# The distance bias made at the start of the program and read back one stage earlier, with the pooling sums placed inside the attention stage

## The chip, the cores and the metric

The kernel runs on one core of a Trainium2 chip. All numbers are fp32. The metric is the device time of one execution in microseconds (us). TensorE does the matrix products (PE in the profile, PEld its weight loads), VectorE (DVE) the elementwise work and the selection, ScalarE (ACT) the activations and the copies out of PSUM, GpSimd (POOL) some memsets, and SyncE (SP) issues most of the transfers.

## The reference, cut to what matters

Three model blocks follow one another on x of 512 x 1024. Only the first is touched. It projects a normalised x into the inputs of three mixers. One is a gated linear attention (`gla`); the other two are those of this change:

```python
# sparse attention, 6 heads of 64, per block of 128 queries
_, idx = lax.top_k(score, topk)                 # score of an indexer, 4 heads of 32; topk = 128
rel = tq[None, :, None] - idx
bias = rb[t5_bucket(rel)]                       # rb: 32 buckets x 6 heads, chosen by distance
logits = logits + jnp.moveaxis(bias, -1, 1)
p = jax.nn.softmax(logits, axis=-1)

# pooling mixer, 4 groups of 64 channels, windows (2, 4, 8, 16) over the positions
outs.append((c - lower) / cnt - ug[:, :, gi])   # c: running sum; lower: c shifted by the window
y = jnp.einsum('btgc,gcd->btgd', pooled, pool_w) * pool_scale

y = jnp.concatenate([y_gla, y_dsa, y_pool], axis=-1)
x = x + jnp.einsum('btc,cd->btd', y, w_out[l])
```

## The kernel before

The program is a row of blocks. Each block gives every engine its own list of instructions, written by hand in order, and ends when all five engines have met at a barrier. Inside a block, engines wait for each other on semaphores alone. In order of time the blocks that matter are `load_x`, a norm, `projection`, `gla`, `dsa_select`, `dsa_attend`, `pool_mix` and `mix_out`.

`load_x` loads x, turns it with TensorE, and gathers some thirty small vectors by transfers that ScalarE's queue issues. SyncE's queue carries the identity, x, and the first three pieces of `early_w`. That is a stream of weight pieces in three slots (`Stream.load`, line 188): a piece is issued when the product that used its slot is done.

`dsa_select` makes the index scores (TensorE, ScalarE), and VectorE picks the top 128 by repeated max and replace. Beside this TensorE and ScalarE work through the twelve pieces of a `Modulation` (`multiply`, line 252; `turn`, line 263), a product of a vector with a large matrix for a later block.

`dsa_attend` needs the bias as a tile of 128 x 512 for each head, in which each partition holds the same row shifted by one. It makes that tile in five steps: TensorE multiplies the table `rb` by a one-hot matrix (lines 837 and 838), VectorE copies the 6 x 640 result to `by_distance` (line 887), SyncE stores it in DRAM (line 824) and waits, reads it back as six overlapping windows plus a matrix `flip` (lines 830 and 831), and TensorE turns the windows around with `flip` (line 843), from where VectorE copies them back. Then come 24 units, one for each query block and head. Of unit i, TensorE makes the logits (852), VectorE adds bias and selection and takes the peak (901 to 906), ScalarE exponentiates (932), VectorE scales (912, 913), TensorE transposes (861), ScalarE copies (940), and TensorE multiplies by v (867). After each unit TensorE also does a half of a piece of a second `Modulation`, and only then the logits of the unit after the next. At the end VectorE multiplies by the gate (917).

`pool_mix` is a block of its own. VectorE makes the four window sums by doubling (lines 971 to 985), TensorE multiplies by `pool_w` (998), VectorE scales and gates (988). `mix_out` multiplies all three mixers' results by `w_out` (1030).

`hT` (`spare` in these functions, `all_hT` in the profile) is a tile of 128 x 8 x 512 that is free for scratch from `gla` to `mix_out`. `Modulation` uses its row 0 and 256 columns of row 1.

Of the kernel before, what the change touches and what calls it, by code (L numbers as in the profile page):

```python
# [17 lines left out]
ALU = mybir.AluOpType  # L18
# [4 lines left out]
P = 128  # L23
T = 512
# [269 lines left out]
def load_x(core, a, xT, ident, ones):  # L294
# [4 lines left out]
    with ExitStack() as ctx:  # L299
        rows, vectors = bufs(nc, ctx, "lx", rows=[P, TT, D], vectors=[P, groups, P])  # L300
# [17 lines left out]
        @block.sync  # L318
        def _(sp):
            sp.dma_start(ident[:], core.const("ident")).then_inc(loaded, 16)  # L320
            sp.dma_start(rows[:], a["x"][0].rearrange("(t p) d -> p t d", p=P)).then_inc(loaded, 16)
            core.early.load(sp, 0)

# [20 lines left out]
        def _(act):  # L344
# [16 lines left out]
            act.wait_ge(small, 64)  # L361

# [341 lines left out]
def dsa_select(core, to, ident, ones, spare, pick, cond, mod):  # L704
# [5 lines left out]
    with ExitStack() as ctx:  # L710
# [82 lines left out]
def dsa_attend(core, to, ident, ones, spare, rel_bias, bias_dram, pick, y, cond, mod):  # L793
# [7 lines left out]
    U = 5 * P  # L801
    with ExitStack() as ctx:
        rb, onehot, by_distance, bias, L, pr, prT, peak, total, flip = bufs(
            nc, ctx, "att", rb=[BUCKETS, DSA_H], onehot=[BUCKETS, U], by_distance=[DSA_H, U],
            bias=[P, DSA_H, T], L=[P, 2, T], pr=[P, 2, T], prT=[P, 2, T], peak=[P, 2], total=[P, 2], flip=[P, P])
        (loaded, table, table_copied, stored, windows, logits, peaked, exped, weights, turned, turned_copied,
         attended, step, gated, flipped, flip_copied) = sems(
            nc, ctx, *(f"att_{s}" for s in ("loaded", "table", "table_copied", "stored", "windows", "logits",
# [11 lines left out]
        def _(sp):  # L820
            sp.dma_start(rb[:], rel_bias).then_inc(loaded, 16)
            sp.dma_start(onehot[:], core.const("bucket", BUCKETS)).then_inc(loaded, 16)
            sp.wait_ge(table_copied, 2)
            sp.dma_start(bias_dram, by_distance[:]).then_inc(stored, 16)
            sp.wait_ge(stored, 16)


            for h in range(DSA_H):
                window = bass.AP(tensor=bias_dram.tensor, offset=h * U, ap=[[1, P], [1, T]])
                sp.dma_start(bias[:, h, :], window).then_inc(windows, 16)  # L830
            sp.dma_start(flip[:], core.const("flip")).then_inc(windows, 16)
# [3 lines left out]
        def _(pe):  # L835
            pe.wait_ge(loaded, 32)
            nc.tensor.matmul(B[6][0:DSA_H, :], rb[:], onehot[:, 0:512], start=True, stop=True).then_inc(table, 1)
            nc.tensor.matmul(B[7][0:DSA_H, 0:U - 512], rb[:], onehot[:, 512:U], start=True,
                             stop=True).then_inc(table, 1)
            pe.wait_ge(windows, 16 * (DSA_H + 1))  # L840
            pe.wait_ge(table_copied, 2)
# [3 lines left out]
            for i in range(N + 1):  # L845
# [8 lines left out]
                if i >= 1:  # L854
# [19 lines left out]
                    else:  # L874
                        beside.multiply(pe, j // 2)

        @block.vector
        def _(dve):
# [5 lines left out]
            for i in range(2):  # L884
                dve.wait_ge(table, i + 1)
                cols = slice(0, 512) if i == 0 else slice(512, U)
                nc.vector.tensor_copy(by_distance[:, cols],
                                      B[6 + i][0:DSA_H, 0:cols.stop - cols.start]).then_inc(table_copied, 1)
# [3 lines left out]
            dve.wait_ge(flip_copied, DSA_H)  # L892
            for i in range(N + 1):
# [14 lines left out]
                if i >= 1:  # L908
# [5 lines left out]
                                            None, ALU.mult).then_inc(weights, 1)  # L914
            for k in range(3):
# [28 lines left out]
def pool_mix(core, to, pool_w, pool_scale, y):  # L944

    nc = core.nc
    B = core.bank
    pu, gate = to["pu"], to["pgate"]
    PAD = max(WINDOWS)
    with ExitStack() as ctx:  # L950
        inv, w, sc, a, b = bufs(nc, ctx, "pool", inv=[P, 2, T], w=[P, 2, 64], sc=[P, 2], a=[P, 2, PAD + T],
                                b=[P, 2, PAD + T])
        loaded, step, pooled, mixed, scaled = sems(nc, ctx, "pool_loaded", "pool_step", "pool_pooled",
                                                   "pool_mixed", "pool_scaled")
        block = ctx.enter_context(nc.Block())

        @block.sync
        def _(sp):
            sp.dma_start(inv[:].rearrange("p k t -> p (k t)"), core.const("inv_count")).then_inc(loaded, 16)
            sp.dma_start(w[:], pool_w.rearrange("(k g) c d -> (g c) k d", g=2)).then_inc(loaded, 16)  # L960
            with nc.allow_non_contiguous_dma("two columns"):
                sp.dma_start(sc[:], columns(pool_scale)).then_inc(loaded, 16)

        @block.vector
# [2000 lines left out]
```

## Time and profile before

| | |
|---|---|
| median of three runs | 4418.44 us (4417.96 to 4422.14) |
| the profiled execution, its own time | 4425.26 us |
| its span | 4423.4 us |
| PE busy | 3726.9 us, 84% |
| DVE busy | 1405.3 us, 32% |
| ACT busy | 697.6 us, 16% |
| the stretch that the change touches | three blocks, 417.4 to 743.2 us, and the first 28.5 us |

Times in the rows below are counted from the start of the span. In a row of a timeline the first number is the start and the second the time from the first instruction's start to the last one's end; brackets hold how long the engine had been idle and what ended that. SPq and ACTq are the queues of instructions that issue transfers, so such a row tells when a transfer was issued, not when it landed.

### The profile page before, as it was taken

To read this page: it belongs to the slowest core of one execution; us is meant where nothing else is said; L and a number is where in the kernel's file an instruction comes from. 1 tells how busy PE (TensorE), PEld (TensorE's weight loads), DVE (VectorE), ACT (ScalarE), POOL (GpSimd) and SP (SyncE) were. 2 spreads that over 40 slices of the span, in tenths; PEclk is the share of its full clock that TensorE was granted. 3 is DMA by queue.
4 is the path that set the end of the run, shared out by engine and by line. 5 is a ranking of instruction groups with operands and counts; after the bars stand their busy time and mean duration, and the time that the engine had idled before them with its cause. 6 is when DMAs were issued, how large, how long until landed. Compare 5 with 4: busy or idle time off the path is not lost. (4 is left out here: it accounts for less than half of the span.)

```text
span 4423.4 us, 32097 instructions
## 1 busy us (share of the span) xinstructions
PE 3726.9 (84%) x11618; PEld 1804.4 (41%) x11618; DVE 1405.3 (32%) x2445; ACT 697.6 (16%) x1294; POOL 231.0 (5%) x241
## 2 busy tenths in 40 slices
PE   7976666799979589999999998595499877889998
PEld 2524233344434234444434343343344566434444
DVE  0005522219322412111121111435825398611011
ACT  1021111101120201001010000303234233110000
POOL 0000000110000100000000000100000255000000
PEclk8985566899989789999999999697799888899999
DMA  2210732372210499999999997311222000212221
GB/s 68 81 59 32 242 125 60 106 260 76 76 48 19 198 344 401 408 400 400 408 400 409 400 407 273 115 58 49 92 74 76 24 6 1 76 59 79 72 76 38
DMA packets 219295, 729.49 MB, mean 165 GB/s; under 512 B 16207, under 2 KB 27104, under 8 KB 184374
## 3 DMA queue, kind: packets, MB, share of 16 engines
q1 hardware_dynamic: 179132, 629.94, 37.7%
q10 hardware_dynamic: 28394, 55.66, 3.6%
q0 software_dynamic: 11664, 42.47, 2.7%
q8 instruction: 68, 1.11, 0.1%
q14 instruction: 37, 0.30, 0.0%
HBM read 678.33 MB, written 49.69 MB: 165 GB/s over the span
## 5 line engine op out<-in xcount | busy, mean ns | idle before, releaser
L1618 PE MATMUL bank<-moe_gu,all_hT 128*128 128x512 f32 x1088 | 471.9, 594 | 0.0
L1117 PE MATMUL bank<-all_hT,early_w 128*128 128x512 f32 x896 | 389.9, 598 | 22.6 <-PEq L135 11.7
L1808 DVE TENSOR_TENSOR all_hT<-bank,moe_bias 128x512 f32<-128x512 f32 x51 | 35.3, 692 | 973.1 <-PE bank L1618 681.1
L1618 PEld LDWEIGHTS bank<-moe_gu,all_hT 128*128 128x128 f32 x1088 | 207.6, 191 | 261.1 <-issue 261.1
L1644 PE MATMUL bank<-moe_dn,moe_rows 128*128 128x512 f32 x544 | 259.8, 639 | 50.0 <-DMA moe_dn<-in_w_dn_dram 49.1
L1117 PEld LDWEIGHTS bank<-all_hT,early_w 128*128 128x128 f32 x896 | 172.0, 192 | 240.6 <-issue 240.6
L1631 PE MATMUL bank<-moe_gu,all_hT 128*64 128x512 f32 x1088 | 236.5, 592 | 1.0 <-issue 1.0
L2331 PE MATMUL bank<-all_hT,hin_w 128*128 128x512 f32 x512 | 223.4, 599 | 13.4 <-DMA hin_w<-in_w_in_dram 13.4
L1117 PE MATMUL bank<-all_hT,late_w 128*128 128x512 f32 x512 | 222.5, 598 | 10.9 <-PEq L372 10.9
L1117 PE MATMUL bank<-b_up,late_w 128*128 128x512 f32 x512 | 220.0, 592 | 2.8 <-PEq L135 2.8
L2634 PE MATMUL bank<-hg_qs,hg_ks 128*128 128x128 f32 x896 | 143.2, 313 | 87.0 <-DVE hg_ks L2580 87.0
L526 PE MATMUL bank<-all_hT,early_w 128*128 128x512 f32 (+3 forms) x432 | 191.1, 604 | 9.9 <-PEq L372 9.9
L1644 PEld LDWEIGHTS bank<-moe_dn,moe_rows 128*128 128x128 f32 x544 | 109.9, 205 | 189.9 <-issue 189.4
L2634 PEld LDWEIGHTS bank<-hg_qs,hg_ks 128*128 128x128 f32 x896 | 127.0, 220 | 100.5 <-DVE hg_ks L2580 100.4
L1195 DVE SCALAR_TENSOR_TENSOR b_conv<-conv_ya,all_table,b_conv 128x512 f32<-128x512 f32 x240 | 159.1, 744 | 0.0
L2331 PEld LDWEIGHTS bank<-all_hT,hin_w 128*128 128x128 f32 x512 | 98.3, 192 | 137.6 <-issue 123.9
L1117 PEld LDWEIGHTS bank<-all_hT,late_w 128*128 128x128 f32 x512 | 98.1, 192 | 135.3 <-issue 135.3
L1978 PE MATMUL bank<-all_hT,si_w 128*128 128x512 f32 x320 | 140.3, 602 | 10.9 <-PEq L372 10.9
L1117 PEld LDWEIGHTS bank<-b_up,late_w 128*128 128x128 f32 x512 | 97.2, 190 | 125.6 <-issue 125.6
L1631 PEld LDWEIGHTS bank<-moe_gu,all_hT 128*64 128x64 f32 x1088 | 81.3, 137 | 152.7 <-issue 152.7
L1657 PE MATMUL bank<-moe_dn,all_hT 128*64 128x512 f32 x544 | 122.4, 602 | 7.0 <-DMA moe_dn<-in_w_dn_dram 4.3
L526 PEld LDWEIGHTS bank<-all_hT,early_w 128*128 128x128 f32 (+3 forms) x432 | 71.2, 166 | 128.1 <-issue 127.6
(541 smaller groups left out, 4157.3 us busy)
## 6 DMA issues: line engine op xcount, KB each, us to landing
moe_gu<-in_w_gu_dram SPq DMA_DIRECT2D x136, 2048.0 KB, 21.4
moe_dn<-in_w_dn_dram SPq DMA_DIRECT2D x68, 2048.0 KB, 23.0
early_w<-in_w_in_dram SPq DMA_DIRECT2D x13, 2048.0 KB, 9.1
expert_rows<-conv_zeros POOLq DMA_DIRECT2D x49, 512.0 KB, 17.2
early_w<-in_w_mod_dram SPq DMA_DIRECT2D x12, 2048.0 KB, 8.1
early_w<-in_ada_w_dram SPq DMA_DIRECT2D x12, 2048.0 KB, 7.9
hin_w<-in_w_in_dram SPq DMA_DIRECT2D x10, 2048.0 KB, 8.4
late_w<-in_w_up_dram SPq DMA_DIRECT2D x8, 2048.0 KB, 9.0
```

The costliest lines, as they stand in the source:

```text
L526: mm = nc.tensor.matmul(out, left, right, start=(k == 0), stop=(k == KT - 1))
L1117: mm = nc.tensor.matmul(B[b][:], w[:, k, m * P:(m + 1) * P], src[:, i * KT + k if stacked else k, :], start=(k == 0), stop=(k == KT - 1))
L1195: nc.vector.scalar_tensor_tensor(out=conv[:, k, :], in0=ya[:, k, bass.ds(j, T)], scalar=conv_w[:, k, bass.ds(j, 1)], in1=conv[:, k, :], op ...
L1618: mm = nc.tensor.matmul(B[bank][:], xb2[:, k, :], gu[:, q, kk, col:col + HALF], start=(k == 0), stop=(k == KT - 1))
L1631: mm = nc.tensor.matmul(B[bank][part, :], xb1[:, k % 4, k // 4, :], gu[:, 4 + q, kk, col + h * HALF:col + (h + 1) * HALF], start=(k == 0), ...
L1644: mm = nc.tensor.matmul(B[2 + n][:], hidT2[:, k * P:(k + 1) * P], dn[:, c, j * D + n * HALF:j * D + (n + 1) * HALF], start=(k == 0), stop= ...
L1657: mm = nc.tensor.matmul(B[4][part, :], hidT1[:, j, c, :], dn[:, c, j * D + h * HALF:j * D + (h + 1) * HALF], start=(c == 0 and j == 0), st ...
L1808: after(vec.tensor_tensor(g, gate[:], bias[0], ALU.add), 1)
L1978: mm = nc.tensor.matmul(B[n % 8][:], w[:, k, (n % 4) * P:(n % 4 + 1) * P], hT[:, k, :], start=(k == 0), stop=(k == KT - 1))
L2331: mm = nc.tensor.matmul(B[n][:], left, right, start=(k == 0), stop=(k == KT - 1))
L2634: mm = nc.tensor.matmul(B[n % 4][:, cols], left[:, cols], right[:, cols], start=True, stop=True)
```

## The change

The bias table is multiplied, copied and stored in DRAM in `load_x`, the windows are read back in `dsa_select`, into rows 2 to 7 of `hT` (and `flip` into its row 1), and `dsa_attend` begins with the turning by `flip`. `pool_mix` is no longer a block: its loads are issued at the start of `dsa_attend`, its VectorE work is cut into eleven pieces of which one follows each unit's scaling, and its product and its scaling stand at the end of `dsa_attend`.

```diff
 def load_x(core, a, xT, ident, ones):
         @block.sync
         def _(sp):
+            sp.dma_start(rb[:], a["rel_bias"]).then_inc(table_loaded, 16)
+            sp.dma_start(onehot[:], core.const("bucket", BUCKETS)).then_inc(table_loaded, 16)
             sp.dma_start(ident[:], core.const("ident")).then_inc(loaded, 16)
             sp.dma_start(rows[:], a["x"][0].rearrange("(t p) d -> p t d", p=P)).then_inc(loaded, 16)
             core.early.load(sp, 0)
+            sp.wait_ge(table_copied, 2)
+            sp.dma_start(a["bias_dram"], by_distance[:]).then_inc(stored, 16)
+            sp.wait_ge(stored, 16)
...
         @block.tensor
         def _(pe):
+            pe.wait_ge(table_loaded, 32)
+            nc.tensor.matmul(core.bank[6][0:DSA_H, :], rb[:], onehot[:, 0:512], start=True, stop=True).then_inc(table, 1)
+            nc.tensor.matmul(core.bank[7][0:DSA_H, 0:U - 512], rb[:], onehot[:, 512:U], start=True,
+                             stop=True).then_inc(table, 1)
             pe.wait_ge(loaded, 32)
             for k in range(KT):
+                if k >= 6:
+                    pe.wait_ge(table_copied, 2)
...
+        @block.vector
+        def _(dve):
+            for i in range(2):
+                dve.wait_ge(table, i + 1)
...
 def dsa_select(...):
             sp.dma_start(hidden[:], core.const("hidden")).then_inc(loaded, 16)
+            for h in range(DSA_H):
+                window = bass.AP(tensor=bias_dram.tensor, offset=h * 5 * P, ap=[[1, P], [1, T]])
+                sp.dma_start(spare[:, 2 + h, :], window).then_inc(windows, 16)
+            sp.dma_start(spare[:, 1, HALF - P:], core.const("flip")).then_inc(windows, 16)
             beside.load(sp)
...
 def dsa_attend(...):
+    bias, flip = spare[:, 2:8, :], spare[:, 1, HALF - P:]
         @block.sync
         def _(sp):
-            sp.dma_start(rb[:], rel_bias).then_inc(loaded, 16)
-            sp.dma_start(onehot[:], core.const("bucket", BUCKETS)).then_inc(loaded, 16)
-            sp.wait_ge(table_copied, 2)
-            sp.dma_start(bias_dram, by_distance[:]).then_inc(stored, 16)
-            sp.wait_ge(stored, 16)
...
+            pool_mix.load(sp)
             beside.load(sp)
...
-            pe.wait_ge(loaded, 32)
-            nc.tensor.matmul(B[6][0:DSA_H, :], rb[:], onehot[:, 0:512], start=True, stop=True).then_inc(table, 1)
...
             pe.wait_ge(windows, 16 * (DSA_H + 1))
-            pe.wait_ge(table_copied, 2)
...
+            pe.wait_ge(peaked, N)
+            pool_mix.multiply(pe)
...
+            sums = pool_mix.sums(dve)
             for i in range(N + 1):
...
                     nc.vector.tensor_scalar(pr[:, j % 2, 0:n], pr[:, j % 2, 0:n], total[:, j % 2:j % 2 + 1],
                                             None, ALU.mult).then_inc(weights, 1)
+                    next(sums, None)
+            pool_mix.scale(dve)
             for k in range(3):
                 dve.wait_ge(attended, N)
...
+class PoolMix:
+    def sums(self, dve):
...
+        nc.vector.memset(b[:, :, 0:pad], 0.0)
+        nc.vector.memset(a[:, :, 0:pad], 0.0)
+        after(nc.vector.tensor_copy(a[:, :, pad:], self.u[:]))
+        yield
+        src, dst = a, b
+        for k, window in enumerate(WINDOWS):
+            tile, row = k // 2, 64 * (k % 2)
+            half = window // 2
+            after(nc.vector.tensor_tensor(dst[:, :, pad:], src[:, :, pad:], src[:, :, pad - half:pad + T - half], ALU.add))
+            yield
+            after(nc.vector.tensor_copy(y[row:row + 64, tile, :], dst[row:row + 64, tile, pad:]))
+            yield
+            src, dst = dst, src
+        dve.wait_ge(self.loaded, 48)
+        after(nc.vector.tensor_tensor(y[:], y[:], self.inv[:], ALU.mult))
+        yield
+        nc.vector.tensor_tensor(y[:], y[:], self.u[:], ALU.subtract).then_inc(self.pooled, 1)
+        yield
```

Three places in the order of instructions. The first is SyncE's list from the start of `dsa_select` on, before the change:

```order
L724 DMA sel_hidden<-consts_dram 128x128
L188 DMA early_w<-in_w_mod_dram 128x8x512 [waits early_product] x9
L188 DMA early_w<-in_ada_w_dram 128x8x512 [waits early_product] x3
L710 UNCONDITIONAL_BRANCH
L819 UNCONDITIONAL_BRANCH [waits barrier_Pool_Activation_PE_DVE_SP_release]
L821 DMA att_rb<-in_rel_bias_dram 32x6
L822 DMA att_onehot<-consts_dram 32x640
L824 DMA bias_by_distance<-att_by_distance 6x640 [waits att_table_copied]
L830 DMA att_bias<-bias_by_distance 128x512 [waits att_stored]
L830 DMA att_bias<-bias_by_distance 128x512 x5
L831 DMA att_flip<-consts_dram 128x128
L188 DMA early_w<-in_ada_w_dram 128x8x512 [waits early_product] x9
```

And the same list with the change:

```order
L749 DMA sel_hidden<-consts_dram 128x128
L752 DMA all_hT<-bias_by_distance 128x512 x6
L753 DMA all_hT<-consts_dram 128x128
L188 DMA early_w<-in_w_mod_dram 128x8x512 [waits early_product] x9
L188 DMA early_w<-in_ada_w_dram 128x8x512 [waits early_product] x3
L735 UNCONDITIONAL_BRANCH
L847 UNCONDITIONAL_BRANCH [waits barrier_Pool_Activation_PE_DVE_SP_release]
L973 DMA pool_inv<-consts_dram 128x1024
L974 DMA pool_w<-in_pool_w_dram 128x2x64
L976 DMA pool_sc<-in_pool_scale_dram 128x2x1
```

The windows moved one block up, behind `sel_hidden`, and the three loads of the pooling mixer stand where the table was. The second place is VectorE's list in `dsa_attend` with the change, from the second unit's peak on; before it had the same rows without those of `pool_a` and `pool_b`:

```order
L916 TENSOR_REDUCE att_peak<-att_L 128x1
L917 TENSOR_SCALAR att_peak<-att_peak 128x1
L923 RECIPROCAL att_total<-att_total 128x1
L924 TENSOR_SCALAR att_pr<-att_pr,att_total 128x128
L986 MEMSET pool_b 128x2x16
L987 MEMSET pool_a 128x2x16
L988 COPY pool_a<-b_pu 128x2x512
L912 SCALAR_TENSOR_TENSOR att_L<-bank,all_hT 128x128
```

Each piece stands between a unit's scaling and the wait for the logits of the unit after the next. The third place is the end of VectorE's list in `dsa_attend` with the change:

```order
L923 RECIPROCAL att_total<-att_total 128x1
L924 TENSOR_SCALAR att_pr<-att_pr,att_total 128x512
L1016 SCALAR_TENSOR_TENSOR b_y_rest<-bank,pool_sc,b_pgate 128x512 x2
L930 TENSOR_TENSOR b_y_rest<-bank,b_dgate 128x512 x3
L831 UNCONDITIONAL_BRANCH
L1053 UNCONDITIONAL_BRANCH
L1057 TENSOR_TENSOR all_xT<-all_xT,bank 128x512 x8
```

The scaling of the pooling mixer, which needs its product, stands ahead of the three gate products, and `mix_out` follows.

## Rows read from the trace of the kernel before

**Rows 1.** Stretches: length; PE, PEld, DVE, ACT, POOL busy; PEclk, DMA share, GB/s.
```profile
417.40:502.40 85.00, 67.46 (x320) 31.04 (x320) 67.57 (x169) 16.19 (x42) 0.28 (x1) 0.56 0.79 275
502.40:528.30 25.90, 9.21 (x16) 3.20 (x16) 5.03 (x8) 1.50 (x2) 0.31 (x1) 0.60 0.42 142
528.30:727.20 198.90, 130.60 (x516) 66.52 (x516) 51.80 (x147) 34.86 (x96) 0.00 (x0) 0.62 0.35 116
727.20:743.20 16.00, 3.69 (x9) 0.89 (x9) 11.17 (x15) 0.00 (x0) 0.00 (x0) 0.54 0.15 37
```

**Rows 2.** Timeline of TensorE at the start of `dsa_attend`.
```profile
508.82 1.87 PE L837 MATMUL bank<-att_onehot,att_rb 32*6 32x512 f32 x2 [6.80 <-DMA att_onehot<-consts_dram]
520.61 6.91 PE L843 MATMUL bank<-att_bias,att_flip 128*128 128x512 f32 x12 [9.49 <-DMA att_flip<-consts_dram]
```

**Rows 3.** Timeline of SyncE's queue, end of `dsa_select` and start of `dsa_attend`.
```profile
487.60 13.10 SPq L188 DMA_DIRECT2D early_w<-in_ada_w_dram  x3
502.48 0.33 SPq L821 DMA_DIRECT2D att_rb<-in_rel_bias_dram  x1
502.85 0.42 SPq L822 DMA_DIRECT2D att_onehot<-consts_dram  x1
511.64 0.32 SPq L824 DMA_DIRECT2D bias_by_distance<-att_by_distance  x1
513.12 2.73 SPq L830 DMA_DIRECT2D att_bias<-bias_by_distance  x6
```

**Rows 4.** Timeline of VectorE inside `dsa_attend`, two units.
```profile
537.37 0.29 DVE L901 SCALAR_TENSOR_TENSOR att_L<-bank,att_bias 128x128 f32<-128x128 f32 x1 [5.91 <-PE bank L852]
541.97 0.29 DVE L901 SCALAR_TENSOR_TENSOR att_L<-bank,att_bias 128x128 f32<-128x128 f32 x1 [3.08 <-PE bank L852]
```

**Rows 5.** Waits, 528 to 720 us: engine, line, for whom: total, times, longest.
```profile
DVE att_L L901 <- PE bank L852: 135.4, 23, 7.9
```

**Rows 6.** Timeline of VectorE, end of `dsa_attend` and `pool_mix`.
```profile
725.09 1.89 DVE L917 TENSOR_TENSOR b_y_rest<-bank,b_dgate 128x512 f32<-128x512 f32 x3 [7.88 <-PE bank L867]
...
727.38 0.68 DVE L973 COPY pool_a<-b_pu 128x1024 f32<-128x1024 f32 x1
728.09 1.23 DVE L979 TENSOR_TENSOR pool_b<-pool_a 128x1024 f32<-128x1024 f32 x1
729.35 0.42 DVE L981 COPY b_y_rest<-pool_b 64x512 f32<-64x512 f32 x1
...
741.30 1.41 DVE L988 SCALAR_TENSOR_TENSOR b_y_rest<-bank,pool_sc,b_pgate 128x512 f32<-128x512 f32 x2 [3.87 <-PE bank L998]
```

**Rows 7.** Timeline of TensorE, end of `dsa_attend` to `mix_out`.
```profile
724.98 1.05 PE L263 MATMUL bank<-all_ones,all_hT 128*128 128x1 f32 x8
737.58 3.67 PE L998 MATMUL bank<-b_y_rest,pool_w 64*64 64x512 f32 x8 [11.55 <-DVE b_y_rest L985]
743.18 6.53 PE L1030 MATMUL bank<-b_y_gla,early_w 96*128 96x512 f32 x8 [1.93 <-PEq L950]
...
753.84 3.60 PE L1030 MATMUL bank<-b_y_gla,early_w 96*128 96x512 f32 x8
```

**Rows 8.** Timeline of `load_x` and the next block: SyncE's and ScalarE's queues, GpSimd.
```profile
6.00 4.62 SPq L188 DMA_DIRECT2D early_w<-in_w_in_dram  x1
...
14.48 1.43 ACTq L352 DMA_DIRECT2D all_skip<-in_d_skip_dram  x2
...
28.57 0.10 POOL L387 MEMSET n_eps<- 128x1 f32 x1 [26.96 <-POOLq L299]
```

**Rows 9.** Tile `early_w`, first 60 us (three transfers).
```profile
DMA to landing us min/median/max: 13.1/17.5/22.3
```

**Rows 10.** Tile `all_skip` (two transfers).
```profile
DMA to landing us min/median/max: 8.3/10.6/12.9
```

**Rows 11.** Tile `att_bias` (six window reads).
```profile
DMA to landing us min/median/max: 3.1/4.0/4.7
```

**Rows 12.** Timeline of VectorE at the start of `dsa_select`.
```profile
419.28 0.29 DVE L771 TENSOR_SCALAR sel_score<-sel_rl,sel_wh 128x128 f32<-128x128 f32 x1 [1.58 <-DMA sel_hidden<-consts_dram]
```

More of the change, by code:

```diff
@@ L299, in load_x @@
     with ExitStack() as ctx:
-        rows, vectors = bufs(nc, ctx, "lx", rows=[P, TT, D], vectors=[P, groups, P])
+        U = 5 * P
+        rows, vectors, rb, onehot, by_distance = bufs(
+            nc, ctx, "lx", rows=[P, TT, D], vectors=[P, groups, P], rb=[BUCKETS, DSA_H], onehot=[BUCKETS, U],
+            by_distance=[DSA_H, U])
+        table_loaded, table, table_copied, stored = sems(
+            nc, ctx, *(f"lx_{s}" for s in ("table_loaded", "table", "table_copied", "stored")))
         loaded, vectors_zeroed, vectors_loaded, turned, copied, ones_set, columns_turned, small = sems(
@@ L701, in _, with dsa_select @@
                                            op1=ALU.mult).then_inc(dve_done, 1)
-def dsa_select(core, to, ident, ones, spare, pick, cond, mod):
+def dsa_select(core, to, ident, ones, spare, pick, cond, mod, bias_dram, windows):
     nc = core.nc
@@ L800, in dsa_attend @@
     N = len(units)
-    U = 5 * P
+    bias, flip = spare[:, 2:8, :], spare[:, 1, HALF - P:]
     with ExitStack() as ctx:
[L803 to L806, printed above, removed]
+        L, pr, prT, peak, total = bufs(
+            nc, ctx, "att", L=[P, 2, T], pr=[P, 2, T], prT=[P, 2, T], peak=[P, 2], total=[P, 2])
+        (logits, peaked, exped, weights, turned, turned_copied,
          attended, step, gated, flipped, flip_copied) = sems(
-            nc, ctx, *(f"att_{s}" for s in ("loaded", "table", "table_copied", "stored", "windows", "logits",
+            nc, ctx, *(f"att_{s}" for s in ("logits",
                                             "peaked", "exped", "weights", "turned", "turned_copied",
@@ new lines, with __init__, load, after @@
+class PoolMix:
+    def __init__(self, core, ctx, to, pool_w, pool_scale, y):
+        nc = core.nc
+        self.core, self.u, self.gate, self.y = core, to["pu"], to["pgate"], y
+        self.sources = core.const("inv_count"), pool_w, pool_scale
+        pad = max(WINDOWS)
+        self.inv, self.w, self.sc, self.a, self.b = bufs(
+            nc, ctx, "pool", inv=[P, 2, T], w=[P, 2, 64], sc=[P, 2], a=[P, 2, pad + T], b=[P, 2, pad + T])
+        self.loaded, self.step, self.pooled, self.mixed, self.scaled = sems(
+            nc, ctx, "pool_loaded", "pool_step", "pool_pooled", "pool_mixed", "pool_scaled")
+    def load(self, sp):
+        inv_count, pool_w, pool_scale = self.sources
+        sp.dma_start(self.inv[:].rearrange("p k t -> p (k t)"), inv_count).then_inc(self.loaded, 16)
+        sp.dma_start(self.w[:], pool_w.rearrange("(k g) c d -> (g c) k d", g=2)).then_inc(self.loaded, 16)
+        with self.core.nc.allow_non_contiguous_dma("two columns"):
+            sp.dma_start(self.sc[:], columns(pool_scale)).then_inc(self.loaded, 16)
+    def sums(self, dve):
+        nc, a, b, y = self.core.nc, self.a, self.b, self.y
+        pad = max(WINDOWS)
+        steps = Count(self.step)
+        def after(instruction):
+            dve.wait_ge(self.step, steps.by(instruction))
+        nc.vector.memset(b[:, :, 0:pad], 0.0)
[16 more added lines that the diff above has]
+        yield
+    def multiply(self, pe):
+        pe.wait_ge(self.loaded, 48)
+        pe.wait_ge(self.pooled, 1)
+        for g in range(4):
+            rows = slice(64 * (g % 2), 64 * (g % 2) + 64)
+            self.core.nc.tensor.matmul(self.core.bank[g // 2][rows, :], self.w[rows, g // 2, :], self.y[rows, g // 2, :],
+                                       start=True, stop=True, skip_group_check=True).then_inc(self.mixed, 1)
+    def scale(self, dve):
+        for tile in range(2):
+            dve.wait_ge(self.mixed, 4)
+            self.core.nc.vector.scalar_tensor_tensor(
+                out=self.y[:, tile, :], in0=self.core.bank[tile][:], scalar=self.sc[:, tile:tile + 1],
+                in1=self.gate[:, tile, :], op0=ALU.mult, op1=ALU.mult).then_inc(self.scaled, 1)
```

73 lines of the change are left out of this document (9 added, 64 removed).

## The prediction

> **What bounds the kernel now.** I read the stretches of the program first. Three stretches hold what the change touches: the selection (85.0 us), the attention (25.9 us of preparation and 198.9 us of units) and the pooling mixer (16.0 us) [rows 1]. No engine is full in the second of these: PE is busy 9.2 of 25.9 us and VectorE 5.0. In the pooling stretch VectorE is busy 11.2 of 16.0 us and PE 3.7 [rows 1]. These are chains, where one engine works at a time.
>
> The timelines show the links. In the attention's preparation PE starts its table product at 508.82, after an idle of 6.80 us for `onehot`, though that transfer was issued at 502.85; then it stands 9.49 us for `flip` and starts to turn the windows at 520.61 [rows 2, 3]. In between lie the store, issued at 511.64, and the windows, issued from 513.12 on [rows 3]. At the other end PE does the last `turn` at 724.98, then waits 11.55 us for VectorE's sums, multiplies for 3.67 us, and starts `mix_out` at 743.18 [rows 7].
>
> In the units between, PE and VectorE take turns. VectorE waits 135.4 us in 23 waits for the logits, since PE does a half of a `Modulation` piece before it makes them [rows 5]. The kernel has barriers between all blocks, so what one of these loses or gains is carried to the end.
>
> **The preparation moves away: -18.1 us.** With the change nothing that PE needs in the attention is made there. The windows are issued at the start of the selection, some 85 us earlier; a window read took 4.7 us at most [rows 11]. So PE can turn them as soon as the block opens. The block opens when SyncE issues its first transfer, 502.48 [rows 3], and I put PE at 502.5. Before it began at 520.61 [rows 2]: 18.1 us go. What is late next is `Modulation`'s first piece. The last three were issued from 487.60 to 500.7 [rows 3] and the first is wanted near 515, so they have landed. The turning itself (twelve products, 6.91 us [rows 2]) stays. Its size hangs on the clock: at the speed of the faster `mix_out` row it would be 12/8 of 3.60 = 5.4 us, and at the granted half the double, 10.8 [rows 7]. I take no change, with bounds -1.5 and +3.9.
>
> **The store in `load_x`: +2.5 us.** This is the part that speaks against the change. Two loads stand ahead of x, which costs 0.33 + 0.42 = 0.8 us of issue [rows 3]. The table product and the copies wait for no weights and are done long before x is turned. But the store is issued on the queue that has just taken three weight pieces. `onehot` shows what that means: issued while a weight piece was on its way, it ended PE's wait 6 us later [rows 2, 3]. The third piece of `load_x` is issued from 6.00 on and lands up to 22.3 us later, at 28.3 [rows 8, 9]. The block ends now at about 28.1, when the last `skip` transfer lands (15.2 plus 12.9), and the next opens at 28.57, 0.5 later [rows 8, 10]. With the change SyncE waits for the store: 28.3, plus 0.8, plus 1.5 for a store on an idle queue (511.64 to 513.12 [rows 3]), plus 0.5 for the barrier gives 31.1, so 2.5 more than 28.57. The low bound is 0: that the store lands before `skip`. The high bound takes 4.7 us for the transfer, the longest window read, in place of 1.5: +5.7 [rows 11].
>
> The trace thus shows a small transfer behind a large one waiting some 6 us. The Trainium skill, "DMA: Bandwidth & Descriptors", section on queues, rings and completion order, says that on each DMA engine the descriptors of one queue are consumed in ring order; by that rule the store cannot start before the weights ahead of it have been read, and the sum gets its 2.5 us, where free overtaking would make the term 0. The trace agrees, as far as the one `onehot` transfer shows it.
>
> **Windows beside the selection: +0.2 us.** They are issued behind `hidden`, for which VectorE waits 1.58 us until 419.28 [rows 12]. If seven transfers right behind it delay it, the selection's scores shift and with them ScalarE's last rectifiers, on which `Modulation` waits. Bounds are 0 and 1.2, the latter the shortest window read (3.1 [rows 11]) less the 1.9 from the block's opening to 419.28 [rows 1, 12]. I take 0.2, near the low end, because `hidden` stays first in the queue. In this block a weight piece is issued only when a product has freed its slot, and the products begin after the scores, so the windows take bandwidth from nothing.
>
> **The sums in the attention: 0.** They are one copy of 0.68, four additions of 1.23, four copies of 0.42 and two more of 1.23 like the additions [rows 6], 9.7 us in eleven pieces, plus two memsets. The longest piece is 1.23. It stands behind a unit's scaling, where VectorE waits for logits, 5.91 us in one early unit and 3.08, the shortest of all, in the next [rows 4]; the mean is 135.4/23 = 5.9 [rows 5]. Each piece fits into the hole two times over, so the cover is PE's half piece of `Modulation`. Without this cover all 9.7 us would be on the path.
>
> **The end of the attention and the pooling block: -10.6 us.** From the end of the last `turn`, 724.98 + 1.05 = 726.03, to `mix_out` at 743.18 there are 17.15 us [rows 7]. With the change the path is: the product, then the scaling 1.41, then the three gates 1.89 [rows 6], then 0.47 of barrier (741.30 + 1.41 to 743.18). The gates now stand behind the scaling, so they count, where before they ran beside PE's last `turn`. The product took 3.72 to the scaling, at a time when PE had stood for 11.55 us [rows 7, 6]; right behind a `turn` it could run at twice that speed, 1.9. I take 2.8 between them: 2.8 + 1.41 + 1.89 + 0.47 = 6.6, and 17.15 - 6.6 = 10.6 us go. Bounds are -9.7 and -11.5. The first eight products of `mix_out` took 6.53 where later ones take 3.60 [rows 7]; as PE will have stood some 4 us again I leave them, with a bound of -2.9.
>
> **Sum.** -18.1 + 2.5 + 0.2 + 0 - 10.6 = -26.0 us. Against the profiled execution this is 4425.3 - 26.0 = 4399.3 (a span of 4397.4). That execution lies 6.8 us above the median of the runs, so for the median I take 4418.4 - 26.0 = 4392.4. All best bounds give -18.1 - 1.5 + 0 + 0 - 11.5 - 2.9 = -34.0, and all worst -18.1 + 3.9 + 5.7 + 1.2 - 9.7 = -17.0: 4384.4 to 4401.4. A difference of some 0.2% (8.8 us) is about what a measurement of this kernel can tell from none.
>
> **Rivals.** *The sums lengthen the units.* VectorE would have to be the last to come at the logits; against it speaks the shortest hole of 3.08 us. It decides from holes under 1.23. Price up to +9.7: 4402.1. Chance 0.06.
>
> *Another wait takes the preparation's place*, for instance ScalarE's table for `activate` or a late window, so that the 18.1 stay. Nothing in the rows names such a wait. The gain is then 7.9: 4410.5, the same as before. Chance 0.03.
>
> *The clock in the units changes.* Both stages run between the two levels: 0.62 in the units, 0.56 in the selection [rows 1], with 0.5 meaning 1.2 GHz. The change shifts these stages and takes out three stretches in which PE stood. If the units fell to 0.56, PE's 130.6 busy us would grow by 0.62/0.56 - 1 = 11%, 14 us: 4406. Chance 0.07. If they rose to 0.70 they would shrink by 15 us: 4378. Chance 0.07. If the units ran at 0.50 throughout and the selection as well, the price is 31.3 + 8.1 = 39 us, and the kernel is slower than before at 4432. That is the case on the other side. It decides from a price of 35 us, so neither stage alone gets there. Both would have to be all slow, and each has fast parts now. Chance 0.02.
>
> The Trainium skill, "TensorE: Matmul & The Clock Gate", part 1, says that the array is throttled by default and that activity releases it. By it the removal of idle stretches leads to the case of 4378 rather than to those of 4406 and 4432; the trace agrees in that the product at 737.58, after a long idle, was slow.
>
> **Numbers.** The forecast's case has a chance of 0.75, with 4384 to 4401 as its own range. From 4383 to 4403 lies this case and that of the longer units, 0.81. Faster: 0.75 + 0.06 + 0.07 + 0.07 less a little for misreading, 0.93. Same: the stayed wait and a little, 0.05. Slower 0.02.
>
> **What the profile of the changed kernel would show.** PE's turning within 0.5 us of the block's opening; the opening of the norm after `load_x` at about 31 instead of 28.57; VectorE's waits for logits shorter by some 10 us in total, with the units' stretch still near 199; `mix_out` some 6.6 us after the last `turn`; no block between. The prediction is wrong if the units' stretch moves by more than 5 us, if `load_x` ends after 34, or if PE waits at the attention's start.

## The result, and the profile after

| | before | changed |
|---|---|---|
| median of five runs | 4418.44 us (4411.71 to 4422.14) | 4395.92 us (4378.44 to 4396.33) |
| profiled execution, own time | 4425.26 us | 4384.45 us |
| its span | 4423.4 us | 4382.6 us |

The ratio of the runs is 0.9936, with a 95% interval of 0.9915 to 0.9958. So the kernel is 0.6% faster, about 28 us, by the interval 19 to 38; the medians differ by 22.5 us. The forecast was 4392.4 us.

The five times of the changed kernel lie 18 us apart, which is too coarse for terms of one or two microseconds. The stages of a trace are finer, since a stage opens at a barrier and GpSimd's first memset shows when. Its timeline with the change (each row the start, the time taken, the line, the tile, and the idle before):

```profile
29.93 0.10 POOL L412 MEMSET n_eps<- 128x1 f32 x1 [28.32 <-POOLq L299]
299.12 0.41 POOL L600 MEMSET gla_S<- 48x384 f32 x1 [269.10 <-POOLq L514]
417.74 0.31 POOL L236 MEMSET all_hT<- 128x256 f32 x1 [118.17 <-POOLq L576]
502.81 0.31 POOL L236 MEMSET all_hT<- 128x256 f32 x1 [84.76 <-POOLq L735]
783.47 0.10 POOL L412 MEMSET n_eps<- 128x1 f32 x1 [280.34 <-POOLq L1032]
```

The first row answers to the 28.57 of [rows 8]: `load_x` ends 1.36 us later. The attention opens at 502.81 where it opened at 502.49. The last row is the opening of the norm behind `mix_out`. In the trace of before the same row reads:

```profile
813.56 0.10 POOL L387 MEMSET n_eps<- 128x1 f32 x1 [310.76 <-POOLq L1013]
```

So 30.1 us are won by here in this pair of traces. TensorE's timeline shows where, and answers to [rows 2] and [rows 7]:

```profile
502.86 7.08 PE L856 MATMUL bank<-all_hT 128*128 128x512 f32 x12 [0.51 <-PEq L735]
510.73 0.49 PE L865 MATMUL bank<-b_dk,b_dq 64*128 64x128 f32 x4 [0.79 <-DVE all_hT L901]
...
708.22 1.05 PE L263 MATMUL bank<-all_ones,all_hT 128*128 128x1 f32 x8
709.20 1.93 PE L1010 MATMUL bank<-b_y_rest,pool_w 64*64 64x512 f32 x8
714.88 5.37 PE L1049 MATMUL bank<-b_y_gla,early_w 96*128 96x512 f32 x8 [3.74 <-PEq L831]
```

The turning of the windows starts 0.05 us after the block opens, where it waited until 520.61. The product of the pooling mixer follows the last `turn` without a wait, where it waited 11.55 us. VectorE's timeline shows a piece of the sums in its hole, and the end:

```profile
521.07 0.29 DVE L924 TENSOR_SCALAR att_pr<-att_pr,att_total 128x128 f32<-128x128 f32 x1
521.27 1.22 DVE L994 TENSOR_TENSOR pool_b<-pool_a 128x1024 f32<-128x1024 f32 x1
525.53 0.29 DVE L912 SCALAR_TENSOR_TENSOR att_L<-bank,all_hT 128x128 f32<-128x128 f32 x1 [3.04 <-issue]
...
711.21 1.41 DVE L1016 SCALAR_TENSOR_TENSOR b_y_rest<-bank,pool_sc,b_pgate 128x512 f32<-128x512 f32 x2 [10.73 <-PE bank L1010]
712.53 1.88 DVE L930 TENSOR_TENSOR b_y_rest<-bank,b_dgate 128x512 f32<-128x512 f32 x3
```

A piece of 1.22 us leaves 3.04 us of idle behind it; the next one that long leaves 2.91. The stretches with the change, in the columns of [rows 1], are cut at the opening of the attention, the first logits, the last `turn`, and the start and end of `mix_out`:

```profile
502.81:510.73 7.92, 7.09 (x13) 2.80 (x13) 4.15 (x6) 1.50 (x2) 0.31 (x1) 0.78 0.87 320
510.73:708.22 197.49, 129.81 (x509) 66.69 (x509) 58.86 (x157) 34.71 (x95) 0.00 (x0) 0.61 0.34 113
708.22:714.88 6.66, 2.92 (x18) 1.47 (x17) 3.20 (x5) 0.16 (x1) 0.00 (x0) 1.00 0.31 129
714.88:783.47 68.59, 63.76 (x144) 27.77 (x144) 5.49 (x8) 0.00 (x1) 0.01 (x1) 0.97 0.05 18
```

And the same four before:

```profile
502.49:528.31 25.82, 9.21 (x16) 3.20 (x17) 5.03 (x8) 1.50 (x2) 0.31 (x1) 0.60 0.42 142
528.31:724.98 196.67, 129.55 (x509) 65.55 (x509) 49.91 (x144) 34.70 (x95) 0.00 (x0) 0.62 0.34 113
724.98:743.18 18.20, 4.72 (x17) 1.83 (x17) 13.05 (x18) 0.16 (x1) 0.00 (x0) 0.60 0.24 80
743.18:813.56 70.38, 64.92 (x144) 28.29 (x144) 5.50 (x8) 0.00 (x0) 0.00 (x1) 0.94 0.06 21
```

The preparation (from the opening to the first logits) lost 17.9 us, the units gained 0.8, the tail (from the last `turn` to `mix_out`) lost 11.5, and `mix_out` lost 1.8. With +0.3 for the later opening these make the 30.1. VectorE carries 9 us more in the units, which got only 0.8 longer. One thing does not fit: the two spans differ by 40.8 us. The other 10.7 us are the subject of the first experiment.

### The profile page after: what moved, and what is told of

It reads as the page before. It is cut to its first block and busy times, and to the rows that moved or that the text cites. A ratio compares the mean times of both kernels' runs of the same rounds, so it can differ in the third digit from the quotient of the medians.

```text
span 4382.6 us, 32087 instructions
## 1 busy us (share of the span) xinstructions
PE 3717.1 (85%) x11618; PEld 1799.6 (41%) x11618; DVE 1401.9 (32%) x2445; ACT 698.0 (16%) x1294; POOL 233.2 (5%) x241
```

## The experiments

Times of a stage are from one trace each. Where a ratio is given it is against runs of before on the same chip. The six variants without a ratio (the sums behind the last unit, both groupings, the store waited for later, the store first, the gates first) ran once each, at 4387.8 to 4403.1 us; such single times tell them neither from the change nor from each other, so they are read by stages alone.

**The changed kernel once more.**

> The changed kernel once more, unchanged. In its first trace the norm after mix_out opens at 783.47 us where before it opened at 813.56, and the rest of the first 866 us keeps that distance (30.1 to 30.4 us), but the span is 40.8 us shorter: 10 us more are lost somewhere between 3640 and 3802 us of before, in the second direction of the HGRN scan, which the change does not touch. Theory (the change is worth what it does in the first block, the rest is chance of the clock in one execution): the norm opens again at 783.5, within 1 us, while the second scan's length (161.6 us before, 149.7 after) comes out anywhere from 147 to 162. Rival (the change shortens the scan, for instance by where code or tiles lie): the scan takes 149.7 again, within 1 us.

Median 4395.69 us against 4424.95, ratio 0.9931 (0.9914 to 0.9948). The norm opened at 785.96, 2.5 later than in the first trace, so the expected 1 us was too narrow. Of this, 1.3 us had come about before the attention opened (504.11 instead of 502.81) and 0.9 in the turning of the windows (8.01 us instead of 7.08). So the gain by this row is 27.6 to 30.1 us. The two scans, in stretches of the first trace and of this one:

```profile
3460.65:3610.45 149.80, 106.29 (x736) 99.09 (x736) 133.20 (x224) 54.23 (x138) 79.52 (x68) 0.86 0.01 4
3610.45:3760.19 149.74, 108.16 (x736) 101.28 (x736) 133.68 (x224) 52.90 (x137) 79.50 (x68) 0.85 0.02 4
```

```profile
3462.58:3623.63 161.05, 109.05 (x736) 102.89 (x736) 135.18 (x224) 53.84 (x138) 77.00 (x69) 0.83 0.01 4
3623.63:3772.52 148.89, 108.05 (x736) 100.98 (x736) 133.84 (x224) 52.94 (x137) 79.56 (x69) 0.85 0.02 4
```

The same program took 161.05 us for the first scan here and 149.80 there. The granted clock was 0.83 against 0.86. The rival, by which the second scan is always 149.7, would stand on this trace alone (148.89), so I took the scans' sum in all thirteen traces of this study: 308.7 before, 299.5 in the first trace of the change, 309.9 in this one, 302.1 in one of the variants below, and 308.7 to 312.5 in the nine others. Among these are kernels with and without each part of the change. Which of the two scans is the long one does go with the kernel: the second in the traces of before and of each part alone, the first in the other eight that have a long one. The sum does not. So 9.1 of the 10.7 us are chance of one execution, and the change's own effect is the 28 to 30 us of the first block.

**Each part alone.** The first kernel keeps `pool_mix` as a block of its own; the second makes the table, the store and the windows in the attention again, into the same scratch tile.

```diff
 # bias only
-            pool_mix.load(sp)
...
-            pe.wait_ge(peaked, N)
-            pool_mix.multiply(pe)
...
-                    next(sums, None)
...
+            dsa_attend(core, to, ident, ones, hT, windows, pick, y_dsa, cond3, core.mod3)
+            pool_mix(core, to, a["pool_w"][0], a["pool_scale"][0], y_pool)
...
 # pooling only, in dsa_attend
+            sp.dma_start(bias_dram, by_distance[:]).then_inc(stored, 16)
+            sp.wait_ge(stored, 16)
+            for h in range(DSA_H):
+                window = bass.AP(tensor=bias_dram.tensor, offset=h * U, ap=[[1, P], [1, T]])
+                sp.dma_start(bias[:, h, :], window).then_inc(windows, 16)
...
```

> Only the bias part: table in load_x, windows beside the selection, the pooling mixer a block of its own as before. Theory (both parts pay, each by its own wait): the first unit's logits at 510.7 as with the whole change, 17.6 us earlier than before; from the last turn to mix_out 18.2 us as before; the norm after mix_out opens at 813.6 - 16.8 = 796.8. Rival (the parts need each other, since the early windows alone only move the idle time): the norm opens within 3 us of before, 811 to 814.

> Only the pooling part: table, store and windows made in the attention block as before (the windows are kept in the scratch tile), the sums beside the units. Theory: logits at 528.3, from the last turn to mix_out 6.7 us instead of 18.2, the norm after mix_out opens at 813.6 - 13 = 800.6, give or take 2 for the clock at the start of mix_out. Rival (the sums lengthen the units by their own 9.8 us): units 9 us longer than 196.7 us, and the norm opens near 810.

| | ratio to before | first logits | units | last turn to `mix_out` | norm opens |
|---|---|---|---|---|---|
| before | 1 | 528.31 | 196.67 | 18.20 | 813.56 |
| bias only | 0.9976 (0.9962 to 0.9990) | 511.41 | 197.50 | 18.20 | 797.12 |
| pooling only | 0.9967 (0.9955 to 0.9979) | 530.15 | 193.84 | 6.66 | 799.14 |
| both, second trace | 0.9931 (0.9914 to 0.9948) | 512.95 | 197.81 | 6.70 | 785.96 |

Both parts pay alone, by 10.6 and 14.6 us of 4425, and together 25 of the 30.5 us that both give, within the intervals. The two norm openings were expected at 796.8 and 800.6. The units of the bias part alone, without any sums in them, took 197.50 us. So the 0.8 us by which the units grew do not come from the sums. The rival of the pooling part, units 9 us longer, fell: with all the sums in them the units were 2.8 us shorter than before, at the same granted clock of 0.62. They lie between these rows:

```profile
530.15 0.49 PE L854 MATMUL bank<-b_dk,b_dq 64*128 64x128 f32 x4 [0.79 <-DVE all_hT L895]
723.99 1.05 PE L263 MATMUL bank<-all_ones,all_hT 128*128 128x1 f32 x8
```

The norm of this part thus opened at 799.14 partly by short units, which the expectation did not have; its logits came 1.85 us later than the expected 528.3. Why the units took 193.8 us here and 196.7 to 197.8 in ten other traces is not shown, and a difference of under 4 us in them cannot be read from one trace.

**The sums behind the last unit.**

```diff
-                    next(sums, None)
+            for _ in sums:
+                pass
             pool_mix.scale(dve)
```

> The changed kernel with all eleven pieces of the sums behind the last unit instead of one behind each of the first eleven units. This prices the cover. Theory (in the changed kernel PE's products hide the sums whole): from the start of the last turn to mix_out about 6.7 + 9.8 less what still lies beside the last unit (some 7 us between VectorE's last scaling and the end of the last turn), plus up to 1.8 because the product follows an idle: 10 to 12 us; units as with the change, 197.5. Rival (the sums cost inside the units as well, by waits for each other): the units get 1 us or more shorter than 197.5.

The tail took 8.82 us (708.84 to 717.66), 2.2 more than with the change, and the units 197.44. The expected 10 to 12 was too much. TensorE's idle ahead of the first products of `mix_out` was as long as with the change (3.71 and 3.74 us), yet they took 6.10 us instead of 5.37. VectorE's timeline shows the last piece, and TensorE's the product behind it:

```profile
709.89 1.23 DVE L1003 TENSOR_TENSOR b_y_rest<-b_y_rest,b_pu 128x1024 f32<-128x1024 f32 x1
```

```profile
708.84 1.05 PE L263 MATMUL bank<-all_ones,all_hT 128*128 128x1 f32 x8
711.27 2.68 PE L1011 MATMUL bank<-b_y_rest,pool_w 64*64 64x512 f32 x8 [1.37 <-DVE b_y_rest L1003]
```

The product began 2.43 us after the last `turn` had begun, where with the change it is 0.98, and took 2.68 instead of 1.93. So only 1.45 us of the 9.8 came onto the path by themselves; the rest lay beside PE's last half piece, transposes and product with v. The prediction's remark that without the cover of the units all 9.7 us would be on the path was too strong. The rival found nothing either: the units are as long without the sums as with them.

**The sums in fewer, longer groups.**

```diff
-                    next(sums, None)
+                    for _ in range(3):
+                        next(sums, None)
```

```diff
-                    next(sums, None)
+                    if j == 0:
+                        for _ in sums:
+                            pass
```

> The changed kernel with three pieces of the sums behind each of the first four units, not one behind each of eleven. The groups take 3.2, 2.1, 2.1 and 2.5 us or so. Theory (a piece costs nothing while it is shorter than VectorE's wait for logits, 3.08 us in the shortest unit): only a group longer than the hole it stands in costs, so the units' 197.5 us grow by less than 1 us. Rival (each piece in the units costs some of its length, by engines queueing behind VectorE): the first four units grow by a good part of the 6.6 us that are newly in them, 3 us or more.

> The changed kernel with all eleven pieces, 9.8 us, in one hole, behind the first unit's scaling. The hole there is 5.9 us long, since PE does a whole Modulation product in it. Theory: the cover is that hole and no more, so the third unit's peak comes 9.8 - 5.9 = 3.9 us later, the units take 201.4 us instead of 197.5, and no later unit gives any of it back. Rival (the cover is loose, later holes take up what one unit loses): units within 1 us of 197.5.

In threes the units took 197.55 us (512.28 to 709.83), as with single pieces. The rival, 3 us or more, fell. The shortest idle left behind a group was 1.34 us:

```profile
524.53 1.22 DVE L995 TENSOR_TENSOR pool_b<-pool_a 128x1024 f32<-128x1024 f32 x1
527.10 0.29 DVE L912 SCALAR_TENSOR_TENSOR att_L<-bank,all_hT 128x128 f32<-128x128 f32 x1 [1.34 <-PE bank L865]
```

All in one hole made them 201.14 us (512.36 to 713.50), 3.6 more, where 3.9 was expected. TensorE's idle ahead of the next transpose says the same, 5.65 us instead of the 1.67 that it has there in the trace of the change:

```profile
527.03 0.47 PE L874 MATMUL bank<-all_ident,att_pr 128*128 128x128 f32 x1 [5.65 <-DVE att_pr L924]
```

So the cover is each unit's hole: what spilled out of this one was not given back by later units.

**The store in `load_x`.** In one kernel the wait for it stands in the next block, and the table lies in a tile that nobody writes before `gla`. In the other the store goes ahead of the weights.

```diff
 # store waited for later
-            sp.wait_ge(stored, 16)
...
+                norm(core, "n1", xT, hT, ones, scratch, ng, loads=lambda sp: sp.wait_ge(core.bias_stored, 16))
...
 # store first
-            core.early.load(sp, 0)
             sp.wait_ge(table_copied, 2)
             sp.dma_start(a["bias_dram"], by_distance[:]).then_inc(stored, 16)
+            core.early.load(sp, 0)
```

> The changed kernel with the wait for the store moved from the end of load_x into the next block (the source of the store lies in a tile that is written only in gla). Theory (the store, queued behind three weight pieces, ends load_x): the next block opens where the last skip transfer allows, 0.4 us after it, about 29.0, instead of 29.9. Rival (the store is not what ends load_x; the two more loads at its start are, since they push all transfers back): it opens at 29.9 again.

> The changed kernel with the store of the table issued ahead of the three weight pieces in load_x, so that only x stands before it. Theory (the store is late because it is queued behind the weights): load_x no longer ends by it, and the next block opens where the skip transfer allows, at 29.0 or a little before, instead of 29.9, as with the later wait (28.93). Rival (holding the weights back until the table is copied, some 4 us, pushes the whole stream of transfers and with it skip): it opens at 30 or later.

The next block opened at 28.93 and 28.98, where the change has 29.93 (29.84 in its second trace). Two later kernels below also have the store first, and they opened at 29.14 and at 29.81:

```profile
29.81 0.10 POOL L412 MEMSET n_eps<- 128x1 f32 x1 [28.20 <-POOLq L299]
```

What is steady is the distance to the landing of the last `skip` transfer, its issue plus the longest of the two times to landing. Where the store goes first or is waited for later the block opened some 0.4 us behind it, in all four traces, as in those of before and of the pooling part alone. With the store last it opened 0.8 to 1.3 us behind it in all seven. So the store is what ends `load_x`. In the kernel of 29.81 `skip` itself landed at 29.4, not at 28.5 to 28.7. The price of the store is 0.9 to 1.0 us by the first two kernels, and 0.6 by the mean of the three with the store first (29.31) against the seven with it last (29.90). The two small loads ahead cost at most 0.4. SyncE's queue with the store first:

```profile
2.12 0.43 SPq L328 DMA_DIRECT2D lx_rows<-in_x_dram  x1
6.08 0.34 SPq L330 DMA_DIRECT2D bias_by_distance<-lx_by_distance  x1
6.46 5.64 SPq L188 DMA_DIRECT2D early_w<-in_w_in_dram  x3
```

and with the change, behind the weights:

```profile
2.59 9.10 SPq L188 DMA_DIRECT2D early_w<-in_w_in_dram  x3
11.74 5.05 SPq L331 DMA_DIRECT2D bias_by_distance<-lx_by_distance  x1
```

The issue alone took 5.05 us there instead of 0.34. By the opening of the attention nothing of this is left to be seen: it lay at 504.09 and 503.08 with these two kernels, and at 502.79 to 504.44 with those that have the store last.

**A shorter tail.** First the three gates ahead of the scaling.

```diff
-            pool_mix.scale(dve)
             for k in range(3):
                 dve.wait_ge(attended, N)
                 nc.vector.tensor_tensor(y[:, k, :], B[4 + k][:], gate[:, k, :], ALU.mult).then_inc(gated, 1)
+            pool_mix.scale(dve)
```

> The changed kernel with VectorE's three gate products ahead of the scaling of the pooling mixer, as they need only the attention's result. Theory (the tail is a chain of turn, product, scaling, gates, and the gates can lie beside turn and product): from the start of the last turn to mix_out 6.66 - 1.88 = 4.8 us. Rival (the gates are not on the chain, the barrier waits for another engine): 6.7 as before.

The tail took 4.87 us, and `mix_out` began with fast products:

```profile
708.20 1.05 PE L263 MATMUL bank<-all_ones,all_hT 128*128 128x1 f32 x8
709.19 1.93 PE L1010 MATMUL bank<-b_y_rest,pool_w 64*64 64x512 f32 x8
713.07 3.67 PE L1049 MATMUL bank<-b_y_gla,early_w 96*128 96x512 f32 x8 [1.95 <-PEq L831]
```

The norm opened at 779.96, 3.5 us before the first trace of the change. The tail's rival, a barrier that waits for another engine, fell: 1.8 of the 1.88 us of the gates were gone. Then this with the store first, and last the store first with PE's product ahead of the last unit's transposes:

```diff
+                if i == N:
+                    pe.wait_ge(peaked, N)
+                    pool_mix.multiply(pe)
                 if i >= 1:
                     j = i - 1
...
-            pe.wait_ge(peaked, N)
-            pool_mix.multiply(pe)
```

> The changed kernel with both improvements, gates ahead of the scaling and the store ahead of the weights. Theory (stages add): from the start of the last turn to mix_out 4.87 us as with the gates alone, the first eight products of mix_out again at 3.7 us, next block after load_x at 29.0, and the norm after mix_out opens 278.2 us after the attention's flips' block opens less 1 of load_x: about 779 to 781 against 783.5 to 786 of the change. Against before the ratio is 0.992 or less. Rival (a faster tail is given back by a colder clock in mix_out): mix_out takes more than 67 us.

> The changed kernel with the store ahead of the weights and PE's product of the pooling mixer ahead of the last unit's transposes, the scaling still ahead of the gates. Theory (PE is full from there to the last turn, so the product keeps its 1.9 us on the path, but the scaling and part of the gates then lie beside PE's work): from the start of the last turn to mix_out 0.1 + 1.89 + 0.47 = 2.5 us instead of 6.66, units 1.9 us longer, in all 2.2 us less than the change. Rival (PE has idle there, waiting for VectorE's scaling): units as before, 197.5.

The first took 4394.28 us, ratio 0.9934 (0.9919 to 0.9949), with the tail at 4.87, the first products of `mix_out` at 3.67, and the norm at 780.15. From the attention's opening to the norm's it has 277.08 us, and the gates alone have 277.17, where the change has 280.66 and 281.85 and three variants with the change's tail have 280.61 to 280.90. These 3.6 us are clear in the stages and below what the runs can tell. The expected ratio of 0.992 or less did not come, though the interval does not rule it out. The rival, a `mix_out` of more than 67 us, fell: 66.8 us. The second took 4391.53 us, ratio 0.9933 (0.9913 to 0.9953): tail 2.46 us and units 199.71, 1.9 longer than in the change's second trace, both as expected. But its `mix_out` started slowly:

```profile
712.59 1.05 PE L263 MATMUL bank<-all_ones,all_hT 128*128 128x1 f32 x8
715.05 6.64 PE L1050 MATMUL bank<-b_y_gla,early_w 96*128 96x512 f32 x8 [1.41 <-PEq L831]
```

Its `mix_out` took 69.69 us, 2.9 more than in the kernel just named and 1.2 more than in the change's second trace (68.50). From opening to opening it has 280.73 us, 1.1 less than that second trace, whose preparation was as long (8.87 and 8.84 us), and not 2.2 less as expected; the first trace of the change has 280.66. Neither variant is shown to be faster than the change by time.

## Why the prediction was right

| step of the prediction | forecast | first trace | second trace |
|---|---|---|---|
| the preparation moves away (start of the turning) | -18.1 | -18.1 | -18.1 |
| the turning, up to the first logits | 0 (-1.5 to +3.9) | +0.2 | +1.1 |
| the store in `load_x`, at its end | +2.5 | +1.4 | +1.3 |
| the same at the attention's opening | | +0.3 | +1.6 |
| windows beside the selection | +0.2 | -0.1 | -0.7 |
| the sums in the attention | 0 | units +0.8 | units +1.1 |
| the end of the attention | -10.6 | -11.5 | -11.5 |
| `mix_out` | 0 (bound -2.9) | -1.8 | -1.9 |
| sum to the norm | -26.0 | -30.1 | -27.6 |

In the sum the store and the windows count by the attention's opening.

The mechanism was right in both halves, and each was shown by taking the other away. Three sizes were off: the store, the tail and `mix_out`, by about 1, 1 and 2 us, all to the good side. That the median came within 3.5 us of the forecast does not confirm the terms, since the interval of the runs (19 to 38 us) is far wider than these errors. The windows cost nothing: VectorE waited 1.57 us for `hidden`, where it had waited 1.58.

The store was over-priced. I had added a whole transfer of 1.5 us behind the third weight piece. With the change that piece, issued from 7.0 on, landed up to 22.4 us later, at 29.4, and the block opened at 29.93, one barrier later. So the store landed with the piece and not after it; that is argued from these two numbers, since the trace shows no landing for the store. The order in the queue, which the row of `onehot` gave, held: with the store ahead of the weights it no longer ended the block. The change holds a check on that row too. In its `load_x` the same `onehot` is issued with no weights ahead of it, and it ended PE's wait 2.1 us later, not 6:

```profile
1.20 0.41 SPq L326 DMA_DIRECT2D lx_onehot<-consts_dram  x1
3.25 1.87 PE L343 MATMUL bank<-lx_onehot,lx_rb 32*6 32x512 f32 x2 [3.25 <-DMA lx_onehot<-consts_dram]
```

The Trainium skill, "DMA: Bandwidth & Descriptors", section on queues, rings and completion order, has the rule of ring order. These rows agree with it, though they do not tell a wait in the ring from a share of busy DMA engines.

Of the 1.4 us of the first trace 0.3 were left when the attention opened, but that is luck of one trace. The norm behind `load_x` and the projection took 269.2 us in it and 270.3 in the second, 270.0 before, and 269.3 to 270.9 in the other ten.

The tail was under-priced. I took 2.8 us for the product, between 1.9 and 3.72. It ran at the fast level, 1.93, since it followed the `turn` at once; the granted clock in the tail was 1.00 where it had been 0.60. `mix_out` began sooner after work, and its first eight products took 5.37 instead of 6.53. Both lay inside the bounds. The Trainium skill, "TensorE: Matmul & The Clock Gate", part 1, has the rule that activity releases the throttle. It pointed this way, and the rows of the change agree; the variant with an idle of 1.41 us and 6.64 us of first products does not. The case that the prediction drew from it, units at 0.70, did not come about.

The sums cost nothing, for the stated reason, a hole longer than the piece. The wait of 3.08 us was not the shortest of all, as the prediction says: the one before the first unit was 0.65, but no piece stands there. The group of three, which still fits, and the group of eleven, which spills by 3.6 us, bound the reason from both sides.

The signs that I had written down came out as follows. PE's turning came within 0.5 us. VectorE's wait for the logits has two rows with the change, 82.2 us in 13 waits and 45.1 us in 10 for which the trace names no releaser (the `issue` above). Together they are 127.3 us, 8.1 less than [rows 5], where some 10 were expected; in the trace with groups of three one row has all 23 and says 126.7. The opening after `load_x` was 29.93 and not 31. `mix_out` came 6.66 us after the start of the last `turn`; I had counted 6.6 from its end, and by that count it was 5.6.

Of the rivals, the lengthened units and the stayed wait fell by the rows above. The units' granted clock was 0.61 against 0.62, so neither of the clock cases in the units came about. The time did move by 9 us in the scans of the third block, for which the prediction had no term. A lower granted clock went with the longer scan, but PE was busy only 2.8 us more in the 11.3 us by which the first one grew (109.05 and 106.29 us), so that the clock is the cause is not shown.

## What to carry to other kernels

Look for stretches in which engines work one after another while the stage beside them has holes: a chain of small steps with no input from that stage can be moved there whole. Cut the moved work into pieces shorter than the shortest hole; a piece was free while it fitted, and of the 4.0 us by which the eleven overran their hole 3.6 were paid. A small store that ends a block should not be issued behind large loads on the same queue (worth 0.6 to 1.0 us at the end of the block here, and nothing that could be seen later), and a gate or copy that is ready early should stand ahead of one that waits.

## What the runs showed of the hardware

One execution of a program can differ from the next by 10 us in a stage that is the same in both. The two scans took 299.5 and 302.1 us in two traces and 308.7 to 312.5 in eleven, at granted clocks of 0.85 and 0.86 in the two, and with one of the two scans at 0.83 in all eleven. Spans of single executions are no measure of a change of this size.

A transfer of the same `onehot` was there 2.1 us after its issue with no weights ahead of it, and 6.0 us after it behind a weight piece. The issue of a small store took 5.05 us behind three weight pieces and 0.34 ahead of them.

The first eight products of `mix_out` are the same in all kernels, and the bias part alone started them as slowly as before:

```profile
721.51 3.68 PE L1005 MATMUL bank<-b_y_rest,pool_w 64*64 64x512 f32 x8 [11.54 <-DVE b_y_rest L992]
727.11 6.52 PE L1037 MATMUL bank<-b_y_gla,early_w 96*128 96x512 f32 x8 [1.92 <-PEq L957]
```

Their time, the idle ahead of them and the time of the eight pooling products ahead of that idle were:

| traces | first eight | idle ahead | pooling products |
|---|---|---|---|
| gates first, gates and store first | 3.67 | 1.95 | 1.93 |
| the change twice, pooling only, threes, both other stores | 5.37 | 3.74 to 3.78 | 1.93 |
| sums behind the last unit | 6.10 | 3.71 | 2.68 |
| before, bias only | 6.52, 6.53 | 1.92, 1.93 | 3.67, 3.68 |
| product before the last unit, store first | 6.64 | 1.41 | 1.93, and 2.8 us of other products behind them |
| all in one hole | 7.06 | 3.75 | 1.93 |

So the length of the idle alone does not set the level. The same idle of 1.9 us stood ahead of 3.67 us where the products before it had run at the fast level, and ahead of 6.5 us where they had run at the slow level after an idle of 11.5 us. That does not settle it either: 5.37 and 7.06 us followed like idles behind like products, and an idle of 1.41 us was followed by a slower start than one of 1.95. What else sets it is open, and no run here was made for it.
